# A two-layer decoder trunk with a 32-expert mixer: expert routing done tile by tile inside the output steps

## The reference

```python
for layer in range(DEPTH):
    u = rmsnorm(h, mix_norm[layer])
    h = h + mixer(u)                       # mLSTM + GLA, or windowed attention
    u = rmsnorm(h, ffn_norm[layer])
    # router: 4 group logits (top 1), 8 expert logits of that group (top 2)
    # weight of an expert: softmax over the groups times softmax over the two
    # expert: (silu(u @ w_gate) * (u @ w_up)) @ w_down, 1024 -> 512 -> 1024
    h = h + hierarchical_moe(u, ...)
return rmsnorm(h, final_norm)
```

## Time and profile before

| | us |
|---|---|
| median of 3 runs (2432.35 to 2438.35) | 2436.44 |
| profiled execution | 2433.56 |
| its span in the trace | 2431.8 |
| layer 0 with its output steps | 0 to 586.5 |
| route stage, layer 0 | 586.5 to 622.9 |
| expert stage, layer 0 (with overflow) | 622.9 to 1253 |
| layer 1 with its output steps | 1253 to 1717.7 |
| route stage, layer 1 | 1717.7 to 1753.9 |
| expert stage, layer 1, overflow and finish | 1753.9 to 2431.8 |

### The profile page before, as it was taken

One profiled execution on the slowest core, in us unless ns is written; L12 is line 12 of the kernel. 1 busy time (PEld: TensorE's weight loads), 2 busy tenths in 40 slices (PEclk: granted clock), 3 DMA queues, 4 the chain that ended last, 5 costly groups with the idle time before them and its releaser, 6 DMA issues. The chain is left out here.

```text
span 2431.8 us, 29766 instructions
## 1 busy us (share of the span) xinstructions
PE 2121.2 (87%) x10467; PEld 1735.8 (71%) x10467; DVE 1553.9 (64%) x1591; ACT 1335.4 (55%) x1648; POOL 419.3 (17%) x381
## 2 busy tenths in 40 slices
PE   6989998985699999999959988899389999999990
PEld 5768876774588777877747867778378777777780
DVE  3551234443688888887845367623488888888885
ACT  4322334541488777777743256622078777777772
POOL 1200001110123222222213400000012222222220
PEclk9989998997799999999979978999699999999995
DMA  3112212113499999999943020000289999999975
GB/s 120 35 44 78 77 53 105 53 61 121 175 371 382 371 361 348 360 362 343 369 177 111 1 78 1 1 27 35 116 313 374 356 354 357 369 360 352 359 280 224
DMA packets 122120, 512.90 MB, mean 211 GB/s; under 512 B 27133, under 2 KB 28218, under 8 KB 87226
## 3 DMA queue, kind: packets, MB, share of 16 engines
q1 hardware_dynamic: 102458, 474.08, 52.7%
q0 software_dynamic: 18432, 33.60, 3.7%
q10 hardware_dynamic: 1152, 4.19, 0.5%
HBM read 495.02 MB, written 50.33 MB: 224 GB/s over the span
## 5 line engine op out<-in xcount | busy, mean ns | idle before, releaser
L1691 DVE TENSOR_TENSOR exp_w_lo<-ring_raw,exp_w_hi 128x2048 fp32r<-128x2048 f32 x384 | 866.4, 2289 | 105.5 <-ACT exp_w_hi L1630 104.9
L1630 ACT ACTIVATE exp_w_hi<-ring_raw 128x2048 fp32r<-128x2048 f32 x384 | 729.0, 1917 | 154.9 <-PE exp_y_out L1579 78.0
L1579 PE MATMUL exp_gate_out<-exp_w_hi,exp_x_hi 128*128 128x512 f32 x512 | 208.2, 407 | 11.8 <-DVE exp_w_lo L1691 10.7
L1579 PE MATMUL exp_y_out<-exp_w_hi,exp_hid_hi 128*128 128x512 f32 x512 | 211.7, 413 | 3.8 <-DVE exp_hid_lo L1706 3.8
L1579 PE MATMUL exp_y_out<-exp_w_lo,exp_hid_hi 128*128 128x512 f32 x512 | 205.4, 401 | 0.0
L1579 PE MATMUL exp_y_out<-exp_w_hi,exp_hid_lo 128*128 128x512 f32 x512 | 204.7, 400 | 0.0
L1579 PE MATMUL exp_gate_out<-exp_w_hi,exp_x_lo 128*128 128x512 f32 x512 | 201.9, 394 | 0.0
L1579 PE MATMUL exp_gate_out<-exp_w_lo,exp_x_hi 128*128 128x512 f32 x512 | 201.7, 394 | 0.0
L1579 PE MATMUL exp_up_out<-exp_w_hi,exp_x_lo 128*128 128x512 f32 x512 | 199.3, 389 | 0.0
L1579 PE MATMUL exp_up_out<-exp_w_hi,exp_x_hi 128*128 128x512 f32 x512 | 199.2, 389 | 0.0
L1579 PE MATMUL exp_up_out<-exp_w_lo,exp_x_hi 128*128 128x512 f32 x512 | 199.2, 389 | 0.0
(11 more groups left out here) (418 smaller groups left out, 4016.1 us busy)
## 6 DMA issues: line engine op xcount, KB each, us to landing
ring_raw<-in_expert_w_gate_dram SPq DMA_DIRECT2D x128, 1024.0 KB
ring_raw<-in_expert_w_up_dram SPq DMA_DIRECT2D x128, 1024.0 KB, 11.7
ring_raw<-in_expert_w_down_dram SPq DMA_DIRECT2D x128, 1024.0 KB, 8.3
l0w_raw<-in_ab_w_in_dram SPq DMA_DIRECT2D x48, 256.0 KB, 2.8
l_q<-y_rows SPq DMA_DIRECT2D x8, 1024.0 KB, 5.1
finish_y<-y_rows SPq DMA_DIRECT2D x8, 1024.0 KB
base_h<-in_x_dram ACTq DMA_DIRECT2D x8, 512.0 KB, 6.9
gate_rows<-l0w_stage SPq DMA_DIRECT2D x16, 256.0 KB, 2.0
```

The source lines that it names most:

```text
L1579: last = nc.tensor.matmul(out, x[:, k0 + k], w[:, k, cols], start=(first and k == 0 and t == 0), stop=(last_unit and k == K - 1 and t == 2))
L1630: nc.scalar.activation(split[split_slot(unit)][0][:], raw[raw_slot(unit)][:], ACT.Copy).then_inc(hi_ready, 1)
L1691: nc.vector.tensor_tensor(lo[:], raw[raw_slot(unit)][:], hi[:].bitcast(F32), ALU.subtract).then_inc(lo_ready[split_slot(unit)], 1)
```

## The change

The block `route` is gone in both layers. Its work is cut up:

- `choose_experts` (DVE) finds group and experts of one tile when its logits are there. In layer 0 `take_logits(w)` moves ahead of `probabilities(t + 1)`, and the choice stands behind `mask_att(t + 1)`, right before the next step's `factors`; in layer 1 both stand together.
- `rank_tokens` and `enter_tokens` (PE) and `place_tokens` (DVE) rank, place and enter one tile. Both layers rank tiles 0 to 5 at once and then tiles 6 and 7 singly, in their last steps, and `make_tables` (DVE) follows at the end.
- Logits come from the un-normed rows: PE turns `h` itself, the router's weights are multiplied by the norm's gain beforehand (POOL), the product has the tokens on the output's partitions, and DVE does `product * scale + bias`. `turn_logits` and `copy_logits` go. The normed row for the gather is made by ACT (`normed`: copy times scale) and POOL (times gain, `normed_rows`) instead of DVE. In layer 0 on ACT `h_root` comes behind `router_cols`; SLOTS goes from 4 to 3.
- Layer 1's `project_out` and `residual` go bank by bank, with the halves of `turn_rows` between them.
- SP loads the first six ring units at the end of the layer's block. In `experts`, ACT and DVE split units 8 and 9 before x is there, DVE instead of POOL clears the two x buffers, and the weights' exponentials are taken there.
- The overflow blocks' tables are worked out in `experts`: `place_rest`, 76 instructions on POOL with a drain between dependent ones, between gather(1) and gather(2), 32 passes on PE behind the last expert's product, and `make_tables` on DVE.

The core of the diff (the new helpers; the parts of `place_rest`; the order on each engine):

```diff
+def choose_experts(v, dve, c, R, logits, t):
+
+
+    far = c["far"][:, 0:N_EXPERTS]
+    v.tensor_reduce(R.g_top, logits[:, t, 0:4], AX.X, ALU.max)
+    dve.drain()
+    v.scalar_tensor_tensor(R.g_flags, logits[:, t, 0:4], R.g_top, c["far"][:, 0:4], ALU.is_ge, ALU.mult)
+    dve.drain()
+    v.tensor_reduce(R.g_idx, R.g_flags, AX.X, ALU.min)
+    dve.drain()
+    v.tensor_scalar(R.masked, c["group_far"][:], R.g_idx, NEG, ALU.not_equal, ALU.mult)
+    dve.drain()
+    v.tensor_tensor(R.masked, R.masked, logits[:, t, 4:36], ALU.add)
+    for k in range(2):
+        dve.drain()
+        v.tensor_reduce(R.top[:, k, t:t + 1], R.masked, AX.X, ALU.max)
+        dve.drain()
+        v.scalar_tensor_tensor(R.flags, R.masked, R.top[:, k, t:t + 1], far, ALU.is_ge, ALU.mult)
+        dve.drain()
+        v.tensor_reduce(R.idx, R.flags, AX.X, ALU.min)
+        dve.drain()
+        v.tensor_scalar(R.hot[:, k, t], far, R.idx, None, ALU.is_equal)
+        if k == 0:
+            dve.drain()
+            v.scalar_tensor_tensor(R.masked, R.hot[:, 0, t], NEG, R.masked, ALU.mult, ALU.add)
+    dve.drain()
+    v.tensor_tensor(R.both[:, t], R.hot[:, 0, t], R.hot[:, 1, t], ALU.add)
+    if t == 0:
+        last = v.memset(logits[:, 0, 4:36], 0.0)
+    else:
+        last = v.tensor_tensor(logits[:, t, 4:36], logits[:, t - 1, 4:36], R.both[:, t - 1], ALU.add)
+    return last
+
+
+def rank_tokens(mm, c, R, logits, t, ranks):
+    mm(ranks[:, N_EXPERTS * t:N_EXPERTS * (t + 1)], c["tri_strict"][:], R.both[:, t], start=True, stop=False)
+    return mm(ranks[:, N_EXPERTS * t:N_EXPERTS * (t + 1)], c["ones"][:], logits[:, t, 4:36], start=False, stop=True)
+
+
+def place_tokens(v, dve, c, R, t, ranks):
+
+    for k in range(2):
+        v.tensor_scalar(R.block_hot[t % 2][:, k], R.hot[:, k, t], c["value"][:, k, t:t + 1], None, ALU.mult)
+    for k in range(2):
+        v.tensor_tensor(R.work, R.hot[:, k, t], ranks[:, N_EXPERTS * t:N_EXPERTS * (t + 1)], ALU.mult)
+        dve.drain()
+        v.tensor_reduce(R.pos[:, k, t:t + 1], R.work, AX.X, ALU.add)
+        dve.drain()
+        last = v.tensor_scalar(R.slot_hot[t % 2][:, k], c["iota"][:], R.pos[:, k, t:t + 1], None, ALU.is_equal)
+    return last
+
+
+def enter_tokens(mm, R, t, made):
+    for k in range(2):
+        last = mm(made, R.slot_hot[t % 2][:, k], R.block_hot[t % 2][:, k], start=(t == 0 and k == 0), stop=(t == 7 and k == 1))
+    return last
+
+
+def make_tables(v, dve, made, rows_y, rows_u, none, table):
+
+    v.tensor_scalar(none, made, 0.0, float(UNUSED + 1), ALU.is_equal, ALU.mult)
+    dve.drain()
+    v.scalar_tensor_tensor(table, made, -1.0, none, ALU.add, ALU.add)
+    dve.drain()
+    v.tensor_copy(rows_y[:], table)
+    dve.drain()
+    return v.tensor_scalar(rows_u[:], rows_y[:], 1, None, ALU.logical_shift_right)
...
+                def place_rest():
+                    g = nc.gpsimd
+                    pos = R.pos[:].rearrange("p k t -> p (k t)")
+                    g.tensor_scalar(limits[:], c["iota"][:, 0:8], float(P), float(P), ALU.mult, ALU.add)
+                    pool.drain()
+                    g.tensor_tensor(above[:, 0:E], bc(R.counts[:], 2, 8), bc(limits[:], 1, E), ALU.subtract)
+                    g.tensor_tensor(above[:, E:], bc(pos, 2, 8), bc(limits[:], 1, N), ALU.subtract)
...
+                    for n in range(N):
+                        g.tensor_scalar(slot_hot[:, n], c["iota"][:], slot[:, n:n + 1], None, ALU.is_equal)
+                        g.tensor_scalar(block_hot[:, n], c["iota"][:, 0:N_OVER], column[:, n:n + 1], value[:, n:n + 1], ALU.is_equal, ALU.mult)
...
                 gather(0, 0)
                 gather(1, 1)
+                place_rest()
                 for e in (2, 3):
                     pool.wait_ge(x_turned_s, e - 1)
                     gather(e, e % 2)
...
+                pe.wait_ge(over_placed, 1)
+                for n in range(N):
+                    last = nc.tensor.matmul(made[:], slot_hot[:, n], block_hot[:, n], start=(n == 0), stop=(n == N - 1))
...
+                make_hi((-1, 8))
+                make_hi((-1, 9))
                 act.wait_ge(shifted, 1)
...
-                    v.tensor_tensor(logits[:, u], Q_[:, 0:36], c["router_b"][:, 0], ALU.add).then_inc(s["logits_made"], 1)
+                    v.scalar_tensor_tensor(logits[:, u], Q_[:, 0:36], scale[:, u:u + 1], c["router_b"][:, 0], ALU.mult, ALU.add).then_inc(s["logits_made"], 1)
...
+                    if 0 <= w < T:
+                        take_logits(w)
+                    if t + 1 < T:
                         probabilities(t + 1)
                         mask_att(t + 1)
...
+                for t in range(T):
+                    if t >= 1:
+                        residual(t - 1, 1)
+                    if 2 <= t + 1 < T:
+                        out_low(t + 1)
+                    if t >= 1:
+                        h_scale(t - 1)
+                    residual(t, 0)
+                    if t == T - 1:
+                        for done in range(6):
+                            place_tile(done)
+                    if t >= 1:
+                        take_logits(t - 1)
+                residual(T - 1, 1)
+                place_tile(6)
+                h_scale(T - 1)
+                take_logits(T - 1)
+                place_tile(7)
```

More of the change, by code:

```diff
@@ new lines, in load_first_units, with moe @@
+def load_first_units(sp, A, layer, raw, raw_ready):
+    for m, (name, e) in enumerate((("expert_w_gate", 0), ("expert_w_up", 0), ("expert_w_gate", 1))):
+        src = A[name][layer, e].rearrange("(p a k) n -> a p k n", p=P, a=2)
+        for half in range(2):
+            s = 2 * m + half
+            sp.dma_start(raw[s][:].rearrange("p (k n) -> p k n", k=4), src[half]).then_inc(raw_ready[s], 16)
+def moe(nc, c, A, layer, R, logits, weight, u_rows, y_rows, raw, raw_ready):
+    with ExitStack() as ctx:
+        Memory(nc, ctx, f"ring{layer}").sb("raw", [P, len(raw), 2048])
+        experts(nc, c, A, layer, R, logits, weight, u_rows, y_rows, raw, raw_ready)
+    experts_over(nc, c, A, layer, R, u_rows, y_rows)
@@ L1866, in layer1 @@
-def layer1(nc, c, A, h, weight, y_rows, logits, router, u_rows):
+                        dve.drain()
+                        choose_experts(v, dve, c, R, logits, w).then_inc(s["chosen"], 1)
+                place_tile(7)
+                dve.wait_ge(s["entered"], T)
+                make_tables(v, dve, entered, R.rows_y, R.rows_u, R.masked, R.flags)
+                dve.wait_ge(s["counted"], 1)
+                v.tensor_copy(R.counts[:], counted)
+def layer1(nc, c, A, h, weight, y_rows, logits, router, u_rows, R, raw_ring, ring_ready):
@@ L2435, in _, with place_tile @@
+                def place_tile(t):
+                    dve.wait_ge(s["ranked"], 1 if t < 6 else t - 4)
+                    if t >= 2:
+                        dve.wait_ge(s["entered"], t - 1)
+                    place_tokens(v, dve, c, R, t, ranks).then_inc(s["placed"], 1)
                 combine(0)
```

1373 lines of the change are left out of this document (693 added, 680 removed).

## The result

The changed kernel takes 2522.39 us (median of 4 runs, 2519.51 to 2524.91) against 2437.39 us for the kernel before beside it: a ratio of 1.0346, 95% interval 1.0317 to 1.0375. It is 85 us slower, where +12.6 was forecast and 2472 was the top of the range. The span of its profiled execution is 2519.2 us, 87.4 more than before.

A forecast was written before the change was run, and what follows sets the result against it. PE was taken to bound layer 0's steady steps and the expert stretches, with little PE work in two route gaps. Layer 0 +10.3 and layer 1 +2.3 gave +12.6: 2446.2 profiled, forecast 2449 us (this case 2437 to 2465; 8 in 10: 2406 to 2472).

The forecast's parts named there:

- Slower: Whole kernel: the chance that the change makes it slower by more than 0.3% (7.3 us), put at 0.58.
- part 5: Expert stretch: place_rest on POOL, held up by DVE's splits, delays x(2); PE stalls 22.7 us, +25 for each layer.
- Rival (a): Expert stretch: POOL's placing finishes in time, stall 4.5 instead of 25 us a layer, 2408 us; chance 0.20.
- Part 3: Layer 0's output steps: choice before the reciprocal +10, h_root behind router_cols +2, added PE stalls and half clock +4.
- The choice before the reciprocal: Layer 0's steps: choose_experts takes 3.9 us on DVE, making the reciprocal 2.5 us late; +10 for four steps.
- rival (c): Layer 0: POOL's multiplication of normed rows also blocks DVE's choose steps, up to 2.3 us a tile; +14, about 2463; chance 0.12.
- The tail of layer 0: Layer 0's end: PE ranks six tiles, waits for DVE's placing and enters them; +8.7, bounds 3 and 13.
- Part 4: Layer 1's output steps: +12 for the last step and +2.5 for the two-bank split and waits between halves.
- The last step's queue: Layer 1's last step: six placings and one tile's logits and choice on DVE before the last residual; +12, bounds 8 and 16.
- The term of +2.5: Layer 1's steps: two-bank split and waits between halves, +0.65 us in six steps, less logit transposes; bounds 0 to 6.
- Part 1: Last residual to expert block: the route stage goes, -36.1 us in layer 0 and -33.9 in layer 1, bounds 3 either side.
- Part 2: Start of the experts: clearing's 1.84 us and some 1.5 us of splitting go, -3.3 in each layer.

The follow-up runs named there:

- e2: The changed kernel with place_rest ahead of gather(0) and the early splits of units 8 and 9 undone: 2527.9 us (two runs, 2517 and 2538).
- e1: The changed kernel without the overflow tables (place_rest only clears the overflow count, its PE passes and make_tables left out): 2452.1 us, 1.0064 of the kernel before.
- e5: e3 with the normed row on ACT moved ahead of router_cols in layer 0: 2483.7 us, 1.0191 of the kernel before.
- e3: The changed kernel with layer 0's choices of tiles 0 to 3 moved behind the second out_low of the next step: 2514.1 us, 1.0303 of the kernel before.
- e7: The changed kernel with place_rest cut into pieces of about 2.5 us over experts 1 to 8 of POOL's loop: 2510.9 us, 1.0315 of the kernel before.
- e6: The changed kernel with residual(t, 0) of layer 1's output steps ahead of out_low and h_scale on DVE: 2506.9 us, 1.0267 of the kernel before.

## Why the prediction was wrong, step by step

**The direction and the decisive part were right, the size was not.** Slower had 0.58. The mechanism of part 5 is what the trace shows: two PE waits on the gathered x, behind a placing stretched by DVE's splits. It was priced 22.7 us and lasts 30.3. The term that was mis-sized in it is the placing's own length: 28 to 30 us where e2 has 36.5, with 15.7 in the 32 one-hot instructions. What its place adds was sized well, 19 us (57 against 38) where it is 20.7. Besides, it began 13.0 us behind the block's start instead of 9.8, and PE wanted the rows at 45.6 instead of 40.3, which gives back 5. With +25 against +32.1 and +27.6 the two terms miss by 10 us together. Rival (a) had 0.20 and is refuted by the rows and by e1.

**Part 3, layer 0's steady steps, is the largest miss.** +16 was forecast, +34.5 came. The choice before the reciprocal was priced right: 4.2 us, of which 1.33 were idle before. Two terms were missing. One is the lock of 2.6 us in each step, which I had as rival (c) with 0.12 and +14 over the whole kernel; it isn't a rival but comes on top. The other is the half clock behind each PE wait: PE is granted 0.90 of full speed over the 34 us, and is busy 28.0 us where e5, with the same work at 1.00, has 25.7. That is 2.3 us a step, where I put 4 us for all steps. A third was hidden in both: the normed row in ACT's queue, which e3 uncovered and e5 removed. PE's idle time in the step went from 0.2 to 6.0 us; these 5.8 us of wait and the 2.3 of clock make the 8.1 us by which the step grew. The credit of some tenths for removed transposes doesn't show: e5's 25.68 us stand against 25.71 before.

**The tail of layer 0**: +8.7 forecast, within its bounds of 3 to 13 where the tail lasts 51.3 us (+10.7, in e1, e2 and e7 with the same code), and +22.8 in the profiled execution. Which of the two comes is luck of a few hundredths of a us, and the forecast didn't have the case. In it PE waits 3.74 us for the choice of tile 5, whose last step again stands against POOL's multiplication, and ranks at the half clock. DVE and then PE:

```profile
589.82 2.87 DVE L132 TENSOR_TENSOR base_logits<-base_logits,l_scratch 128x32 f32<-128x32 f32 x1
...
592.74 0.41 PE L137 MATMUL l_pair<-l_scratch,base_tri_strict 128*128 128x32 f32 x2 [3.74 <-DVE base_logits L132]
```

**Part 4, layer 1**: +14.5 forecast, +31.7 measured. The last step's queue was right (+11.7, of 89.4 us behind at the last residual and 77.7 at the one before it, forecast +12). The steps before it were not. From the end of tile 0's complete residual to tile 6's are 86.2 us in the kernel before and 100.6 in the changed one, +14.4 where I had +2.5. The other 5.7 lie ahead of tile 0's residual (358.2 us from the overflow block instead of 352.5); e1, with the same code there, takes 350.7, so they are no price of the change that a run shows.

PE's account over all steps, from the end of tile 0's product to the last residual (windows 1602 to 1703.7 of the kernel before, 1665.6 to 1793.1 of the changed one, 1666.9 to 1781.9 of e6): 101.7 us grew to 127.5. More work is 6.9 us (101.2 busy before, 108.1 in e6 at 0.99), mostly the rank and entering passes of six tiles, and one router product with some transposes. In the kernel before these last two lag the projection by one and two tiles, and their end lies behind the last residual; there I counted it as saved in part 1, and didn't count that it now lies in the steps. The clock took 8.3 more (116.4 busy), and waits the remaining 10.6, 5.7 of them in the last step's queue. The term of +2.5 had the waits between the halves about right (0.65 us a step; one of 1.95 and five of 0.67 to 0.68 came). It failed by leaving out the work and the half clock.

**Part 1** misses by 3.8 us in each layer, just outside its bounds of 3. Of that 2.3 and 2.6 us are the lock once more: one instruction of tile 7's choice meets POOL's multiplication of the last normed row and lasts 2.50 us in layer 0 (636.16) and 2.86 in layer 1 (1799.12). **Part 2** failed: -3.3 twice came out at +0.5. The 1.84 us of clearing weren't saved at all, since `gather(0)` waits for DVE's clearing as it did for POOL's: from the block's start to the gather's issue are 3.1 us before and 3.2 now. The splitting saved 3.0 us between transposes and first product (4.3 instead of 7.3), twice what I had put. Against that the rows come 3.4 us later: 1.2 in the gather's issue, which the early splits stand against on the very port that I had made the point of part 5, and some 2.1 behind it, beside ring loads.

**The range** took the lock in as one case among others. The bounds of single terms were too narrow in part 3, where I had a row for the clock's fall and didn't multiply it by the number of steps in which my own sum made PE wait.

## What to carry to other kernels

An edit that fills an engine's idle time on the critical chain must be priced with everything that a wait of PE brings behind it: here 5.8 us of wait a step cost another 2.3 us of half clock, and two moves of order, of which neither removed an instruction, gave 39 us back. Before moving work to POOL read not its busy share but its round: it was 17% busy, and its chain of scatter, wait, gather and wait was as long as PE's round, so that even three instructions a round cost time. Where a few hundredths of a us decide whether two engines block each other for 2.9, a profile of one execution shows one of two outcomes, and it takes several to see both. When steps are shifted to run without lag, the work that used to lie behind the last result is in the steps and may not be booked as saved there.

## What the runs showed of the hardware

A POOL instruction of 32 or 16 elements lasts 0.20 to 0.23 us alone and 2.26 to 2.31 us beside DVE's splits, and the reverse holds as well: a DVE addition of 32 elements lasts 0.19 us, and 2.76 us when it starts 0.14 us behind a POOL multiplication of 2.85 us. In two executions with the same code the DVE addition came 0.01 us (0.19 us long) and 0.03 us (2.87 us long) behind POOL's start. The Trainium skill, "SBUF — State Buffer", section "Who interferes with whom", says that the loser is blocked for the whole instruction; the traces agree, in both directions.

In layer 1 a PE wait as short as 0.68 us, behind sixteen passes of 36 columns (1757.20 to 1759.75), was followed by windows granted 0.50. It was so in two steps of five with that wait, and in none of e6, where the steady steps have the same passes without it and stay at 1.00. And the same 208 PE instructions of layer 0's tail took 51.3 us in one execution and 63.4 in another, at 0.87 and 0.73, with a wait of 1.04 us in the one and 3.74 in the other.

Behind an indirect transfer POOL's next dependent step waits, whatever it is: 6.70 us before a copy of two elements in e7, 3.12 us at 664.29 in the changed kernel, where it is shortest in the rows shown.
